# Hybrid mixer and expert block: first loads on two DMA queues, the u weights in five pieces, ScalarE's table loaded ahead

## The reference

```
h  = RMSNorm(x)
p  = h @ W_in        # columns: conv x | conv B | conv C | u | gate_a | gate_b
ya = W_conv_out(B * dwconv3_causal(C * x_conv))
yb = GLU(gelu(Re(C s_t) + D u_t)),  s_t = A_bar s_{t-1} + B_bar u_t
x  = x + W_o(sigmoid(gate_a) * ya + sigmoid(gate_b) * yb)
x  = x + HierMoE(RMSNorm(x))     # 32 experts, top-1 group, then top-2 experts inside it
out = RMSNorm(x)
```

## Time and profile before

| | us |
|---|---|
| runs | 722.07, 722.08, 724.77 |
| the profiled execution's own time | 723.69 |
| its span, first to last instruction | 722.0 |
| TensorE matmuls busy | 558.9 (77%) |
| DVE busy | 206.8 (29%) |
| ScalarE busy | 70.4 (10%) |
| GpSimd busy | 39.8 (6%) |

### The profile page before, as it was taken

One profiled execution on the slowest core, in us unless ns is written; L12 is line 12 of the kernel. 1 busy time (PEld: TensorE's weight loads), 2 busy tenths in 40 slices (PEclk: granted clock), 3 DMA queues, 4 the chain that ended last, 5 costly groups with the idle time before them and its releaser, 6 DMA issues.

```text
span 722.0 us, 7544 instructions
## 1 busy us (share of the span) xinstructions
PE 558.9 (77%) x3241; PEld 333.3 (46%) x3241; DVE 206.8 (29%) x443; ACT 70.4 (10%) x132; POOL 39.8 (6%) x68
## 2 busy tenths in 40 slices
PE   8999999999999989899384584566548248457755
PEld 7888888888886646354141141123114014112411
DVE  4799886959512144000010010000001001000002
ACT  3010011111110012100000000000000000000102
POOL 5001111111100011000000000000000000000000
PEclk9999999999999999999796688779679669677889
DMA  9960803363269666999999999999999999999993
GB/s 339 425 268 18 332 1 120 113 242 139 86 270 401 232 235 261 364 432 426 430 428 428 430 427 428 430 428 427 428 429 426 433 428 428 431 426 430 426 426 161
DMA packets 19043, 242.44 MB, mean 336 GB/s; under 512 B 2368, under 2 KB 2496, under 8 KB 4544
## 3 DMA queue, kind: packets, MB, share of 16 engines
q1 hardware_dynamic: 18432, 239.83, 79.8%
q10 hardware_dynamic: 576, 2.10, 0.8%
HBM read 240.87 MB, written 1.05 MB: 335 GB/s over the span
## 4 chain that ended last, share of the span: by engine, by line
PE 54%; DMA 41%; DVE 2%; issue 2%; ACT 0%; POOL 0%; SPq 0%; DVEq 0%; PEldq 0%; POOLq 0%; ACTq 0%
PE bank L1114 27%; DMA ring<-in_w_down 13%; DMA ring<-in_w_gate 12%; PE bank L1364 8%; DMA s_region<-in_w_up 4%; DMA x_region<-in_w_up 4%; PE bank L1372 4%; DMA ring<-in_w_up 4%; PE bank L1246 4%; DMA ring<-in_last_halves 3%; PE bank L1126 2%; PE bank L1413 2%; PE bank L1331 1%; PE bank L1216 1%; PE bank L1231 1%
## 5 line engine op out<-in xcount | busy, mean ns | idle before, releaser
L1364 PE MATMUL bank<-ring,z_region 128*32 128x512 f32 x688 | 118.5, 676 | 63.5 <-DMA ring<-in_w_gate 14.9
L1114 PE MATMUL bank<-x_region,ring 128*128 128x256 f32 x640 | 142.2, 381 | 0.0
L1114 PEld LDWEIGHTS bank<-x_region,ring 128*128 128x128 f32 x640 | 120.4, 190 | 20.9 <-issue 5.1
L1364 PEld LDWEIGHTS bank<-ring,z_region 128*32 128x32 f32 x688 | 33.6, 122 | 123.5 <-issue 123.5
L1372 PE MATMUL bank<-ring,m_region 128*32 128x512 f32 x240 | 55.5, 749 | 26.6 <-DMA ring<-in_w_down 16.0
L1038 DVE TENSOR_TENSOR z_region<-z_region,bank 128x512 f32<-128x512 f32 x8 | 8.2, 1027 | 209.2 <-PE bank L1364 197.1
L1364 PE MATMUL bank<-x_region,z_region 128*32 128x512 f32 x80 | 44.9, 725 | 10.7 <-DMA ring<-in_w_up 10.7
L1042 DVE COPY m_region<-bank 128x512 f32<-128x512 f32 x8 | 5.5, 691 | 139.3 <-PE bank L1372 111.3
L1372 PE MATMUL bank<-s_region,m_region 128*32 128x512 f32 x64 | 36.9, 741 | 8.6 <-DMA ring<-in_w_down 8.6
L1364 PE MATMUL bank<-rot_region,z_region 128*32 128x512 f32 x64 | 37.6, 755 | 6.8 <-DMA ring<-in_w_up 6.8
L1331 PE MATMUL bank<-conv_region,h_region 128*128 128x128 f32 x256 | 33.9, 288 | 4.7 <-issue 4.0
(11 more groups left out here) (240 smaller groups left out, 570.0 us busy)
## 6 DMA issues: line engine op xcount, KB each, us to landing
ring<-in_w_gate SPq DMA_DIRECT2D x26, 2048.0 KB, 34.5
ring<-in_w_up SPq DMA_DIRECT2D x17, 2048.0 KB, 33.8
ring<-in_mix SPq DMA_DIRECT2D x16, 2048.0 KB, 9.7
ring<-in_w_down SPq DMA_DIRECT2D x15, 2048.0 KB, 35.0
ring<-in_first SPq DMA_DIRECT2D x8, 2048.0 KB, 12.6
s_region<-in_w_down SPq DMA_DIRECT2D x4, 2048.0 KB, 36.2
x_region<-in_w_up SPq DMA_DIRECT2D x4, 2048.0 KB, 36.8
rot_region<-in_w_up SPq DMA_DIRECT2D x4, 2048.0 KB, 35.8
```

What stands on the lines that cost most here:

```text
L1114: ins = MM(dst, w[:, k, n * P:(n + 1) * P], rhs[:, k, :], start=k == 0, stop=k == kn - 1)
L1364: ins = MM(bank[to][quarter(e), :], xT[:, k, quarter(e)], of_expert[e][:, FF * k:FF * k + FF], start=k == 0, stop=k == KD - 1)
```

## The change

The x pieces and the columns are issued by ScalarE's queue, x piece 0 ahead of the columns. SyncE begins with the u weights, in five pieces of 1, 1, 2, 2 and 2 values of k instead of four pieces of 2, and then goes on as before. ScalarE, having issued, waits for the memset of `halfneg` (a new semaphore) and makes an activation of two elements per partition, whose result is overwritten later, so that its table is loaded there. TensorE waits for the u pieces by their new bounds, and spreads rstd after k = 3 instead of k = 4. DVE makes hT before the chain of coefficients instead of after it.

```diff
-U_PIECES = 4
+X_PIECES = 4
+U_PIECES = ((0, 1), (1, 2), (2, 4), (4, 6), (6, 8))
...
+        halves_set = sem("halves_set")
...
         def _(sp):
-            sp.dma_start(cols[:], columns[:]).then_inc(cols_in, 16)
-
-            def first_piece(c):
-                sp.dma_start(w8(U_U)[:, 2 * c:2 * c + 2, :].rearrange("p k n -> p (k n)"),
-                             mix[U_U, :, 1024 * c:1024 * c + 1024]).then_inc(u_in[c], 16)
-
-            for c in range(U_PIECES):
-                sp.dma_start(x_raw[:, 2 * c:2 * c + 2, :].rearrange("p k t -> p (k t)"), x_columns[c]).then_inc(x_cols_in[c], 16)
-                if c == 0:
-                    first_piece(0)
-            for c in range(1, U_PIECES):
-                first_piece(c)
+            for (k0, k1), landed in zip(U_PIECES, u_in):
+                sp.dma_start(w8(U_U)[:, k0:k1, :].rearrange("p k n -> p (k n)"),
+                             mix[U_U, :, 512 * k0:512 * k1]).then_inc(landed, 16)
...
-            nc.gpsimd.memset(halfneg[:], -0.5)
+            nc.gpsimd.memset(halfneg[:], -0.5).then_inc(halves_set, 1)
...
+            for piece in range(X_PIECES):
+                if piece == 1:
+                    act.dma_start(cols[:], columns[:]).then_inc(cols_in, 16)
+                act.dma_start(x_raw[:, 2 * piece:2 * piece + 2, :].rearrange("p k t -> p (k t)"), x_columns[piece])\
+                    .then_inc(x_cols_in[piece], 16)
+            act.wait_ge(halves_set, 1)
+            nc.scalar.activation(stat[:, 0:2], halfneg[:], ACT.Copy)
...
+            dve.wait_ge(row_ready, 1)
+            dve.wait_ge(h_raw_ready, KD)
+            for piece in range(X_PIECES):
+                V.tensor_tensor(hT[:, 2 * piece:2 * piece + 2, :], h_raw[:, 2 * piece:2 * piece + 2, :],
+                                rstd_row.unsqueeze(1).to_broadcast([P, 2, T]), ALU.mult).then_inc(hT_ready, 2)
 
             link(V.tensor_tensor(c(8), are, are, ALU.mult))
...
             link(V.tensor_tensor(c(15), c(12), c(9), ALU.mult))
-
-            dve.wait_ge(row_ready, 1)
-            dve.wait_ge(h_raw_ready, KD)
-            for piece in range(U_PIECES):
-                V.tensor_tensor(hT[:, 2 * piece:2 * piece + 2, :], h_raw[:, 2 * piece:2 * piece + 2, :],
-                                rstd_row.unsqueeze(1).to_broadcast([P, 2, T]), ALU.mult).then_inc(hT_ready, 2)
...
             for k in range(KD):
-                if k % 2 == 0:
-                    pe.wait_ge(u_in[k // 2], 16)
+                for (k0, _), landed in zip(U_PIECES, u_in):
+                    if k == k0:
+                        pe.wait_ge(landed, 16)
...
-                if k == 4:
+                if k == 3:
                     pe.wait_ge(diag_ready, 1)
```

More of the change, by code:

```diff
@@ L166, in block_kernel @@
         gate_b = ring[:, MIX_RING, 0:KD * T].rearrange("p (k t) -> p k t", k=KD)
-        squares = ring[:, MIX_RING, 0:KD * T].rearrange("p (c n) -> p c n", c=U_PIECES)
+        squares = ring[:, MIX_RING, 0:KD * T].rearrange("p (c n) -> p c n", c=X_PIECES)
         square_sum = ring[:, MIX_RING, KD * T:KD * T + 2 * T]
@@ L242, in block_kernel @@
         rstd = sem("rstd")
-        x_cols_in = [sem(f"x_cols_in{i}") for i in range(U_PIECES)]
-        u_in = [sem(f"u_in{i}") for i in range(U_PIECES)]
+        x_cols_in = [sem(f"x_cols_in{i}") for i in range(X_PIECES)]
+        u_in = [sem(f"u_in{i}") for i in range(len(U_PIECES))]
         h_raw_ready = sem("h_raw_ready")
@@ L1130, in _ @@
                 if k == 2:
-                    pe.wait_ge(square_step, 2 * U_PIECES - 1)
+                    pe.wait_ge(square_step, 2 * X_PIECES - 1)
                     for b in range(TB):
@@ L1539, in laid_out @@
     halves = last[KF - 1].reshape(P, PACK, 2, 512).transpose(2, 0, 1, 3)
-    x_columns = one["x"].reshape(T, U_PIECES, 2, P).transpose(1, 3, 2, 0).reshape(U_PIECES, P, 2 * T)
+    x_columns = one["x"].reshape(T, X_PIECES, 2, P).transpose(1, 3, 2, 0).reshape(X_PIECES, P, 2 * T)
     return {"x": inputs["x"], "x_columns": x_columns, "columns": columns, "mix": mix, "s5_b": s5_b.reshape(P, -1), "s5_c": s5_c.reshape(P, -1),
```

## The result

The changed kernel takes 725.87 us (median of 20 runs, 724.87 to 729.67), the kernel before 723.89 (20 runs, 721.92 to 725.07). The ratio is 1.0040 with a 95% interval of 1.0027 to 1.0052: 2.9 us slower (2.0 to 3.8), outside the range of 719.8 to 723.8. So 1.8 of the 4.5 us between the forecast's 721.4 and the measured 725.87 belong to the base and not to the change; with the ratio on 722.08 the result would still have been 725.0.

A forecast was written before the change was run, and what follows sets the result against it. The mixer was taken as bound by TensorE, the experts by their weight stream. TensorE's side gave 0.75 us and the stream 0.75; not adding, they gave 0.7 off 722.08: 721.4 us, range 719.8 to 723.8.

The forecast's parts named there:

- Part 1: First loads on two queues: full transfer load begins 0.45 us earlier, x1 lands at 6.7 and the columns at 5.0.
- rival C: First loads: ScalarE's queue gets less than half, x3 lands at 11.7, diag late, projection 1.6 us later; 723.7 us; 16%.
- Part 2: ScalarE's first table load: runs from 3.1 to 4.4 under the transfers, so TensorE starts at 5.5, 1.0 us earlier.
- The clock: First 24 u matmuls: 1.86 us too long at half clock rate after an idle gap; half of it taken as regained.
- Part 3: Rstd row after k = 3: TensorE waits 1.0 us for diag; u projection ends at 22.75, a gain of 0.75 us.
- Part 4: hT ahead of the coefficient chain: brings nothing by itself; the delayed chain is covered by 8 us.
- The third weight unit: Load needed by c0: only 0.40 us of slack, landing near 29.3, so c0 begins at most 0.75 us earlier.
- Point C's decision: Diag before the rstd row: the slower case decides if diag is ready later than 16.1, x3 landing after about 10.1.
- the prediction's own sign: Front to end: the 0.7 us shift carries through; wrong if the shift at 34 us differs from that at 309 us.
- rival A: First loads: two queues fill the slow opening, 420 instead of 286 GB/s from 3 to 6 us; 720.1 us; 14%.

The follow-up runs named there:

- e6: The changed kernel with POOL's rstd power ahead of the decay's power; ratio to the kernel before 1.0028 (1.0011 to 1.0046).
- e7: The changed kernel itself, run and profiled again; ratio to the kernel before 1.0039 (1.0025 to 1.0053).
- e10: The changed kernel with hT behind the coefficient chain again; ratio to the kernel before 1.0047 (1.0029 to 1.0064).
- e11: The changed kernel without the early activation that loads the table; ratio to the kernel before 1.0031 (1.0017 to 1.0044).
- e4: The changed kernel with the rstd row after k = 4 again; ratio to the kernel before 1.0013 (1.0001 to 1.0025).
- e2: The kernel before with only x and the columns moved to ScalarE's queue; ratio to the kernel before 1.0041 (1.0028 to 1.0054).
- e5: The kernel before with ten warm-up matmuls instead of seven; ratio to the kernel before 1.0000 (0.9986 to 1.0015).
- e8: Changed kernel with x0 heading SyncE's queue, columns ScalarE's, u in eight pieces, rstd's power first, row after k = 4, second state array behind unit 3; ratio 0.9996.
- e12: The version e8 with the second state array in its old place; ratio to the kernel before 0.9996 (0.9984 to 1.0009).
- e9: The changed kernel with u in two pieces, k = 0 and k = 1 to 7 (14 KB rows); ratio to the kernel before 1.0116 (1.0094 to 1.0137).
- e1: The changed kernel with x, columns and u on one queue, SyncE's, in merged order; ratio to the kernel before 1.0002 (0.9991 to 1.0014).
- e3: The changed kernel with u in eight pieces of one k, 2 KB rows on both queues; ratio to the kernel before 1.0018 (1.0005 to 1.0031).

## Why the prediction was wrong

**The step that failed** is in Part 1: "If two queues share the engines evenly, x1 is complete when 0.58 + 0.52 = 1.10 MB have moved: the same. So x1 lands 0.45 us earlier, at 6.7". The queues do not share bytes evenly but rows (216 against 214 from 6 to 9 us, with 0.41 and 0.77 MB). The sum has a slip too: even shares would be 0.58 + 0.58 = 1.16 MB, some 0.1 us more, which is not what failed. x1 landed at 9.1, the columns at 5.9 (5.0 forecast), and x3 at 13.4 (9.3 with even shares). This is rival C's mechanism, which had 16%. There too the size was too small: x3 at 11.7 and 1.6 us in all, where the profiles show 13.4 and 12.2 and 2.1 to 3.4 us. C took the 3.2 MB from x1's landing at 0.42 MB/us and subtracted 0.45 us for the earlier start. Neither held: DMA moved 395 GB/s from 6 to 9 us and 393 from 9 to 12, and x0 landed at 4.9 instead of 4.0.

**Part 2, the table**: it was ready at 4.72 (4.4 forecast); TensorE began at 6.62 instead of 5.5, because of the columns. So a correct edit met the failed step.

**The clock** was the term of 1.86 us, of which the forecast took half. Matmuls in the profile after, in us, busy (count), granted clock, DMA share, GB/s:

```profile
9.50:11.00 1.50, 1.50 (x8) 1.00 1.03 401
...
15.50:17.00 1.50, 1.50 (x8) 0.63 0.89 382
```

The first 24 took 5.42 us here (as in e6), at 2.4 GHz nearly throughout, and 7.1 in e7, e10 and e11, after idle gaps of 1.4 to 2.0 us in all five. The quick ones end at 12.04 and TensorE waits 2.9 us for the squares; after that the granted clock falls to 0.63 in the mean of the stretch and k = 3 takes 3.52 us instead of 1.78. The slow ones meet no wait there, and one at diag. The forecast's half of 1.86 us lies between the two and is what neither shows.

**Part 3, the row after k = 3**: the forecast wait of 1.0 us was 1.4 in e7, by the mechanism given (POOL's L511 ahead of rstd's power). In the profile of the result most of it hid behind the clock's fall. The e4 interval (1.0001 to 1.0025) lies just under that of the changed kernel (1.0027 to 1.0052): the place is worth about 1 to 2 us of the loss, in line with the 1.5 us between e4's and e7's projections. So the loss of the changed kernel is the late x together with this place; e2 shows that the split loses as much without the place, by the late columns. Point C's decision at diag after 16.1 was right: it was 19.2 and 17.9.

**Part 4, hT**: nothing, as forecast (e10).

**The third weight unit**: it landed at 29.3, as forecast, but TensorE came too late to wait for it. e5, e8 and e12 showed the wait.

**From 34 us to the end**: e2 and e9 carry their shift to the time (3.2 and 8.3 us against 3.0 and 8.4 by the ratios). In the profile of the result 3.37 us at 34 us were 1.8 at 310 us (311.70 against 309.93 in the chains) and 2.6 at the end. By the prediction's own sign, a shift at 309 us that differs from the one at 34, its step from the front to the end did not hold in size either. 1.1 us went at the router, where the kernel before ran its transposes at a lower clock. The first row is of the kernel before, the second, in a fence of its own, of the changed one:

```profile
269.00:272.00 3.00, 2.29 (x9) 0.53 0.99 426
```

```profile
272.00:275.00 3.00, 1.74 (x12) 1.00 1.02 437
```

Whether that belongs to these executions or to the change is not shown: these transposes are quick in both profiles of the changed kernel and in e1, e6 and e8 to e12, and slow in the one of the kernel before and in e2 to e5. The rest stays open, and so does why the 0.7 to 1.3 us of e5, e8 and e12 do not show in the ratios; their intervals would allow most of it.

## What to carry to other kernels

A second queue is not only a second issuer: it changes who is served first. Put against a transfer that is wanted early only rows that are no longer than its own, and order both queues so that what is wanted together stands at the same place in each. Even so ordered, two queues were no faster here than one. Before moving the first loads, find the last transfer that the first long chain needs, here the last quarter of x through squares and two powers, and not only the one that the first matmul waits for.

## What the runs showed of the hardware

The two queues of this core were served in turns of one row each: 15 rows of 14 KB against 15 of 432 bytes in half a microsecond (e9), 214 against 216 in 3 us (the changed kernel). Transfers of 128 rows at the same place landed within 0.5 us of one another in most pairs (at most 0.9), with sizes of 54 KB against 1.8 MB and 256 KB against 2 MB. The Trainium skill, "DMA: Bandwidth & Descriptors", section Queues, rings and completion order, has each engine go round the queues packet by packet, with some 9 to 17 descriptors in a typical packet. The going round agrees with the runs; turns of that many rows do not show, since e9's are of one row.

Two queues hardly opened faster than one. From 4 to 6 us the changed kernel, e2, e3 and e4 moved 325 to 346 GB/s against 258 in the kernel before, but from 2 to 4 us 219 to 240 against 256. Over rival A's own stretch, 3 to 6 us, it was 292 in the changed kernel against 286, where A had assumed 420.

The granted clock in the profile's windows is 1.00 in the kernel before from 7 to 8.5 us, where the spacing of the matmuls is that of 1.2 GHz, and 0.63 in the changed kernel where the same spacing returns. Early in an execution the spacing is the better witness.
